# Query norms kept as token columns, and the sliding attention's query projections moved ahead of its units

## What is computed

```python
def _rms_norm(x, g):
    y = x * lax.rsqrt(jnp.mean(x * x, axis=-1, keepdims=True) + 1e-6)
    return y * g

# layer 0: two attentions with 16 query heads of 64 channels, causal, 512 keys
aq = _rms_norm(aq, qn_a); ak = _rms_norm(ak, kn_a)
bq = _rms_norm(bq, qn_b); bk = _rms_norm(bk, kn_b)
logits = q . k * HEAD_DIM ** -0.5 - slope[h] * dist      # -inf where dist < 0
p = softmax(logits)

# layer 1: sliding attention, 16 query heads, 4 key heads, window of 128, a sink per head
q = _rms_norm(q, qn_c); k = _rms_norm(k, kn_c)
logits = q . k * HEAD_DIM ** -0.5 - slope[h] * dist      # dist in 0..127
p = softmax(concat([logits, sink]))[..., :-1]
```

## Time and profile before

| | us |
|---|---|
| three runs | 2853.36, 2854.61, 2854.35; median 2854.35 |
| the profiled execution's own time | 2861.86 |
| its span, first to last instruction | 2860.1 |
| mean granted TensorE clock | 0.962 |
| busy share: PE, PEld, DVE, ACT, POOL | 94%, 75%, 41%, 37%, 43% |
| layer 0's projection and picks (VectorE's last pick ends) | about 50 to 266 |
| layer 0's attention | 266 to 381 |
| layer 1's chunk 6 projected | 863.23 |
| layer 1's units, first bias to the first matmul of the output projection | 869.46 to 998.20 |

### The profile page before, as it was taken

How to read it: one execution, slowest core, us unless ns; L and a number is a source line. 1 busy time by engine, 2 the same in 40 slices (tenths; PEclk the granted TensorE clock), 3 DMA queues, 4 the chain that set the end, 5 groups by cost and what they waited for, 6 DMA issues and landing times.

```text
span 2860.1 us, 34092 instructions
## 1 busy us (share of the span) xinstructions
PE 2682.9 (94%) x13037; PEld 2130.8 (75%) x13037; DVE 1175.7 (41%) x1698; ACT 1058.9 (37%) x1705; POOL 1235.3 (43%) x652
## 2 busy tenths in 40 slices
PE   6997889999998799999999999999999996999998
PEld 5665567888874478888788888888888762788886
DVE  3288633222147633221236655233321497433312
ACT  3332643332236533332345555333322322433321
POOL 2322533544433235444345655444444485344442
PEclk8998999999999899999999999999999997999998
DMA  8654512332320013323221211222322210132321
GB/s 270 215 167 143 175 45 74 97 108 92 98 75 30 30 59 103 103 88 102 82 74 59 74 60 53 93 91 92 99 96 96 69 64 15 61 116 88 99 96 55
DMA packets 275965, 265.14 MB, mean 93 GB/s; under 512 B 20268, under 2 KB 274829, under 8 KB 275853
## 3 DMA queue, kind: packets, MB, share of 16 engines
q1 hardware_dynamic: 275853, 263.59, 29.1%
HBM read 261.47 MB, written 2.10 MB: 92 GB/s over the span
## 4 chain that ended last, share of the span: by engine, by line
PE 80%; DVE 13%; ACT 3%; issue 2%; SPq 1%; POOL 0%; DMA 0%; DVEq 0%; ACTq 0%
PE bank L1240 20%; PE bank L1241 20%; PE bank L1242 20%; DVE bank L2364 3%; PE bank L980 1%; PE bank L982 1%; PE bank L981 1%; DVE score L2702 1%; PE bank L1264 1%; PE bank L971 1%; PE bank L973 1%; PE bank L972 1%; PE bank L1002 1%; PE bank L1266 1%; PE bank L1265 1%
## 5 line engine op out<-in xcount | busy, mean ns | idle before, releaser
L844 POOL TENSOR_TENSOR w_lo<-w_raw,w_hi 128x1024 fp32r<-128x1024 f32 (+1 forms) x364 | 863.7, 2382 | 1281.4 <-ACT w_hi L1875 746.1
L1240 PE MATMUL bank<-h_hi,w_hi 128*128 128x512 f32 x1632 | 643.8, 394 | 19.1 <-DVE h_lo L2513 12.4
L1241 PE MATMUL bank<-h_lo,w_hi 128*128 128x512 f32 x1632 | 639.5, 392 | 0.0
L1242 PE MATMUL bank<-h_hi,w_lo 128*128 128x512 f32 x1632 | 639.1, 392 | 0.0
L1875 ACT ACTIVATE w_hi<-w_raw 128x1024 fp32r<-128x1024 f32 (+1 forms) x232 | 233.2, 1019 | 482.5 <-PE bank L1242 437.5
L1240 PEld LDWEIGHTS bank<-h_hi,w_hi 128*128 128x128 f32 x1632 | 309.5, 190 | 88.8 <-issue 19.6
L1241 PEld LDWEIGHTS bank<-h_lo,w_hi 128*128 128x128 f32 x1632 | 309.3, 190 | 65.7 <-issue 1.7
L1242 PEld LDWEIGHTS bank<-h_hi,w_lo 128*128 128x128 f32 x1632 | 309.1, 189 | 64.9
L1240 PE MATMUL bank<-a_hi,w_hi 128*128 128x512 f32 x704 | 273.9, 389 | 0.0
L1241 PE MATMUL bank<-a_lo,w_hi 128*128 128x512 f32 x704 | 273.9, 389 | 0.0
L1242 PE MATMUL bank<-a_hi,w_lo 128*128 128x512 f32 x704 | 273.9, 389 | 0.0
(11 more groups left out here) (369 smaller groups left out, 4362.2 us busy)
## 6 DMA issues: line engine op xcount, KB each, us to landing
ada_w<-in_ada_w_dram SPq DMA_DIRECT2D x96, 512.0 KB, 6.1
w_raw<-in_ffn_gate_dram SPq DMA_DIRECT2D x22, 1024.0 KB, 5.2
w_raw<-in_ffn_up_dram SPq DMA_DIRECT2D x22, 1024.0 KB, 5.3
w_raw<-in_ffn_w_gate_dram SPq DMA_DIRECT2D x22, 1024.0 KB, 5.3
w_raw<-in_ffn_w_up_dram SPq DMA_DIRECT2D x22, 1024.0 KB, 5.2
w_raw<-in_ffn_down_dram SPq DMA_DIRECT2D x16, 1024.0 KB, 5.1
w_raw<-in_ssm_w_in_dram SPq DMA_DIRECT2D x16, 1024.0 KB, 5.2
w_raw<-in_ffn_w_down_dram SPq DMA_DIRECT2D x16, 1024.0 KB, 4.9
```

Of the source, the lines that this page charges most:

```text
L844: pool.tensor_tensor(w_lo[parity][:, 0:nk, half], w_raw[parity][:, 0:nk, half], w_hi[parity][:, 0:nk, half].bitcast(F32), ALU.subtract).th ...
L1240: pe.matmul(dst[m][:], hi, src_hi(k0 + k), start=first and k == 0, stop=False)
L1241: pe.matmul(dst[m][:], hi, src_lo(k0 + k), start=False, stop=False)
L1242: ins = pe.matmul(dst[m][:], lo, src_hi(k0 + k), start=False, stop=last and k == nk - 1)
```

## The change

The query norms are no longer applied to the queries. ScalarE copies the raw chunk times the gain (which holds the factor -1/8) into the query tile, which frees the bank (`q_copied`, `o_copied`). TensorE sums the squares with the tokens on the partitions: four pieces of the squares are stationary, two columns of the ones move, and the result is 128x8 (four token tiles by two heads). ScalarE takes the root of 128x8 into `q_sigma`. VectorE makes -1/sigma (`q_minus`) and slope times sigma, in four small instructions. In the units the bias is scaled by the column slope times sigma, the exp takes the column -1/sigma as its scale, and one more VectorE instruction on 128x2 rescales the minimum. Keys are treated as before. In layer 1 all chunks 7 to 11 are projected ahead of the unit loop, their squares, roots and splits too, and nothing of them is left in it. The sums of a query chunk are now written to the chunk's own bank, behind its copy. The columns lie where `log_decay` lies, which is used much later.

```diff
-                low_half(6)
+                for j in range(6, 12):
+                    low_half(j)
                 for s in range(U):
                     even_out(s)
-                    for j in o_ends(s):
-                        low_half(j)
...
             def sums(j):
-                take(2, o_root, j + 1)
+                b = 2 if j < KV_HEADS else O_BANK[j]
+                take(b, o_root, j + 1)
                 pe.wait_ge(o_squared, j + 1)
-                pe.matmul(bank[2][:], head_ones[:], sq[j % 2][:], start=True, stop=True).then_inc(o_summed, 1)
+                if j < KV_HEADS:
+                    pe.matmul(bank[b][:], head_ones[:], sq[j % 2][:], start=True, stop=True).then_inc(o_summed, 1)
+                    return
+                for i in range(NT):
+                    ins = pe.matmul(bank[b][:, 2 * i:2 * i + 2], sq[j % 2][:, P * i:P * i + P], head_ones[:, 0:P:HD],
+                                    start=True, stop=True)
+                ins.then_inc(o_summed, 1)
...
                 if k == 0:
-                    take(b, o_normed, j + 1)
+                    take(b, o_copied, j - 3)
                     pe.wait_ge(w_split, 2 * n + m + 1)
...
             def scores(u):
                 hp, i, w = o_tile(u)
                 k0 = P * max(i - 1, 0)
-                pe.wait_ge(o_normed, 5 + hp)
+                pe.wait_ge(o_normed, KV_HEADS)
+                pe.wait_ge(o_copied, hp + 1)
...
             sums(2)
-            half_cm(n0 + 3, 0, take(O_BANK[4], o_normed, 5))
+            half_cm(n0 + 3, 0, take(O_BANK[4], o_copied, 1))
             sums(3)
-            half_cm(n0 + 3, 1, take(O_BANK[5], o_normed, 6))
+            half_cm(n0 + 3, 1, take(O_BANK[5], o_copied, 2))
             sums(4)
-            half_cm(n0 + 4, 0, take(O_BANK[6], o_normed, 7))
+            half_cm(n0 + 4, 0, take(O_BANK[6], o_copied, 3))
             sums(5)
+            for j in range(7, 12):
+                for f in range(8 * (j - 7), 8 * (j - 7) + 8):
+                    query_part(f)
+                sums(j - 1)
+            sums(11)
             for s in range(U + O_LAG + 1):
-                fill = list(range(o_upto(s), o_upto(s + 1)))
                 if s < U:
                     scores(s)
-                for f in fill[:1]:
-                    query_part(f)
                 if O_LAG <= s < U + O_LAG:
                     turn(s - O_LAG)
-                for f in fill[1:]:
-                    query_part(f)
-                if s == 0:
-                    sums(6)
-                for j in o_ends(s - 1):
-                    sums(j)
                 if O_LAG + 1 <= s < U + O_LAG + 1:
                     weigh(s - O_LAG - 1)
...
                     pe.wait_ge(sq_ready, z + 1)
+                    if 1 <= r - qk_root0 <= 8:
+                        for i in range(NT):
+                            ins = pe.matmul(bank[4][:, 2 * i:2 * i + 2], sq[z % 2][:, P * i:P * i + P], head_ones[:, 0:P:HD],
+                                            start=True, stop=True)
+                        ins.then_inc(sq_summed, 1)
+                        return
                     pe.matmul(bank[4][:], head_ones[:], sq[z % 2][:], start=True, stop=True).then_inc(sq_summed, 1)
...
-                            if part[m] == "qk":
+                            if part[m] == "q":
+                                dst.append(take(banks[m], q_copied, qk + m))
+                            elif part[m] == "qk":
                                 dst.append(take(banks[m], qk_normed, qk0 + qk + 1 + (m if part[0] == "qk" else 0)))
...
-            EVEN_PARTS = [("qk", "plain"), ("bv",), ("plain", "plain"), ("plain", "plain"), ("qk", "qk"), ("qk", "qk"),
-                          ("qk", "qk"), ("qk", "qk"), ("qk", "qk"), ("qk", "qk"), ("tok", 256), ("tok", 256)]
+            EVEN_PARTS = [("qk", "plain"), ("bv",), ("plain", "plain"), ("plain", "plain"), ("q", "q"), ("q", "q"),
+                          ("q", "q"), ("q", "q"), ("qk", "qk"), ("qk", "qk"), ("tok", 256), ("tok", 256)]
...
                 act.activation(sq[j % 2][:], bank[O_BANK[j]][:], ACT.Square).then_inc(o_squared, 1)
+                if j >= KV_HEADS:
+                    act.activation(cq[:, j - 4, :], bank[O_BANK[j]][:], ACT.Copy, scale=qk_gain[:, 4:5]).then_inc(o_copied, 1)
                 round_half(n + 2, m)
 
             def root_of(j):
                 act.wait_ge(o_summed, j + 1)
+                if j >= KV_HEADS:
+                    act.activation(q_sigma[:, j - KV_HEADS, :], bank[O_BANK[j]][:, 0:2 * NT], ACT.Sqrt, bias=eps_col[1e-6][:],
+                                   scale=1.0 / HD).then_inc(o_root, 1)
+                    return
...
                 for t_ in range(2):
                     c = (2 * u + t_) % 32
-                    act.activation(o_prob[u % 4][:, w * t_:w * t_ + w], o_neg[u % 3][:, w * t_:w * t_ + w], ACT.Exp, scale=-1.0,
+                    act.activation(o_prob[u % 4][:, w * t_:w * t_ + w], o_neg[u % 3][:, w * t_:w * t_ + w], ACT.Exp,
+                                   scale=q_minus[:, hp, 2 * i + t_:2 * i + t_ + 1],
                                    bias=least[:, c // 16, c % 16:c % 16 + 1],
                                    accum_out=total[:, c // 16, c % 16:c % 16 + 1]).then_inc(o_exp, 1)
...
             root_of(5)
+            for j in range(7, 12):
+                square(j)
+                root_of(j - 1)
+            root_of(11)
             for s in range(U + O_LAG + 1):
                 if O_LAG <= s < U + O_LAG:
                     copy_turned(s - O_LAG)
-                if s == 1:
-                    root_of(6)
-                for j in o_ends(s - 1):
-                    root_of(j)
                 if s >= O_LAG + 1:
                     round_y(s - O_LAG - 1)
                 if s < U:
                     prob_exp(s)
-                for j in o_ends(s):
-                    square(j)
...
+                    if 1 <= j <= 8:
+                        act.activation(q_sigma[:, j - 1, :], bank[4][:, 0:2 * NT], ACT.Sqrt, bias=eps_col[1e-6][:], scale=1.0 / HD
+                                       ).then_inc(root_done, 1)
+                        return
...
                             act.activation(sq[z % 2][:], bank[b][:], ACT.Square).then_inc(sq_ready, 1)
+                            if part[m] == "q":
+                                to, g = (bq[:, qk - 1, :], 2) if qk <= 4 else (aq[:, qk - 5, :], 0)
+                                act.activation(to, bank[b][:], ACT.Copy, scale=qk_gain[:, g:g + 1]).then_inc(q_copied, 1)
...
-                link(dve.reciprocal(root[j % 2][:], root[j % 2][:]))
-                if j < KV_HEADS:
+                if j >= KV_HEADS:
+                    hp = j - KV_HEADS
+                    link(dve.reciprocal(q_minus[:, hp, :], q_sigma[:, hp, :]))
+                    dve.tensor_scalar(q_minus[:, hp, :], q_minus[:, hp, :], -1.0, None, ALU.mult)
+                    by_head = q_sigma[:, hp, :].rearrange("p (i t) -> p i t", t=2)
+                    for t_ in range(2):
+                        ins = dve.tensor_scalar(by_head[:, :, t_], by_head[:, :, t_], slope[2 * hp + t_], None, ALU.mult)
+                else:
+                    link(dve.reciprocal(root[j % 2][:], root[j % 2][:]))
                     ins = dve.scalar_tensor_tensor(out=ck[:, j, :], in0=bank[b][:], scalar=qk_gain[:, 5:6], in1=root[j % 2][:],
-                                                   op0=ALU.mult, op1=ALU.mult)
-                else:
-                    ins = dve.scalar_tensor_tensor(out=cq[:, j - 4, :], in0=bank[b][:], scalar=qk_gain[:, 4:5], in1=root[j % 2][:],
                                                    op0=ALU.mult, op1=ALU.mult)
                 ins.then_inc(o_normed, 1)
...
+                dve.wait_ge(o_normed, 5 + hp)
...
                 for t_ in range(2):
-                    ins = dve.scalar_tensor_tensor(out=neg[:, w * t_:w * t_ + w], in0=dist_i, scalar=slope[2 * hp + t_],
+                    ins = dve.scalar_tensor_tensor(out=neg[:, w * t_:w * t_ + w], in0=dist_i, scalar=q_sigma[:, hp, 2 * i + t_:2 * i + t_ + 1],
                                                    in1=bank[o_score_banks(u)[t_]][:, 0:w], op0=ALU.mult, op1=ALU.add)
                 ins.then_inc(o_biased, 1)
                 dve.wait_ge(o_biased, u + 1)
                 c = (2 * u) % 32
                 lc = least[:, c // 16, c % 16:c % 16 + 2]
                 link(dve.tensor_reduce(lc, neg[:, 0:2 * w].rearrange("p (t k) -> p t k", t=2), AX_X, ALU.min))
+                link(dve.scalar_tensor_tensor(out=lc, in0=lc, scalar=-1.0, in1=q_minus[:, hp, 2 * i:2 * i + 2], op0=ALU.mult,
+                                              op1=ALU.mult))
                 dve.tensor_tensor(lc, lc, neg_sink[:, 2 * hp:2 * hp + 2], ALU.min).then_inc(o_least, 1)
...
-            for j in range(6):
+            for j in range(12):
                 normed(j)
             for s in range(U + O_LAG + 1):
                 if s < U:
...
```

(30 more changed lines are left out.)

## The result

The changed kernel is slower. Its median is 2873.3 us (seven runs, 2870.4 to 2876.1) beside 2857.1 us for the kernel before (seven runs, 2853.4 to 2864.3), a ratio of 1.0054 with a 95% interval of 1.0042 to 1.0065. A second set of its runs gave 2871.0 us and 1.0048 (1.0035 to 1.0060). The forecast was 2847.3 us, range 2839 to 2860.

The account below looks back on a forecast made before the run. TensorE was taken as bound (busy 94% of the span), VectorE's work paid in a few stages only. Layer 1 gains 7.3 us, layer 0 gains 1.6 and loses 1.9: 2854.35 - 7.0 = 2847.3 us, range 2839 to 2860.

Parts of the forecast that it names:

- rival 2: Layer 1's loop: clock stays at half where values are made, costing 18 us instead of 3, total 2862; chance 0.13.
- signs that I named: Prediction wrong if steps average over 2.6 us, bank waits far exceed 2.3, or attention grows over 5 us.
- The chunks ahead, to 904.9: Layer 1 ahead of the loop: first bias moves from 869.46 to 904.9, adding 35.4 us.
- 3 x (2.3 + 5.50): Layer 1, chunks 9 to 11: each waits 2.3 us for its bank, then takes 5.50 us of products.
- The sum in the loop, 71.3 us: Layer 1's unit loop: steps of 2.23 or 2.02 us, 0.34 more with `low_y`, 71.3 us to the last bias.
- The column scalars replace constants; I cost them at nothing: Layer 1's unit loop: scalars read from columns instead of constants add no time.
- The clock in the loop, 3 us: Layer 1's loop: half clock slows two of twelve steps with values by 1.5 us each; bounds 0 and 18.
- Layer 0's projection, -1.6 us: Ahead of layer 0's attention: VectorE starts the A keys at 193.46 instead of 195.03, gaining 1.6 us.
- Layer 0's attention, +1.9 us: Layer 0's 32 units: the added 128x2 instruction, 0.19 us each, is paid in a third, losing 1.9 us.
- ten units: Layer 0's attention: ten of 32 units have the added instruction on the path, an estimate between the ends.
- Rival 3: Layer 0's attention: added instruction, held up by GpSimd, costs 8.8 us instead of 1.9, total 2854.2; chance 0.17.
- Held up by GpSimd: Layer 1: new VectorE instructions wait for GpSimd's splits, 2.4 us ahead of the loop, 0.15 per 128-key step.

Follow-up runs that it names:

- banks experiment: Changed kernel with chunks 7 to 11 in banks 7, 3, 4, 0 and 1, so none waits for an earlier root: 2858.8 us, ratio 1.0004 to before.
- fed loop: Changed kernel with idle TensorE products in layer 1's unit loop, three per step without values, one with: 2864.6 us, ratio 1.0028 to before.
- its part alone: Kernel before with only layer 1's edits, query chunks ahead of the units and column scalars: 2860.7 us, ratio 1.0017.
- layer 0's part alone: Kernel before with only layer 0's edits, token-column query norms, column scalars and the added 128x2 instruction: 2865.0 us, ratio 1.0023.

## Why the prediction was wrong

**Direction.** I gave slower by over 0.2% a chance of 0.10 and by one mechanism, rival 2. It came by others. By the runs of each part alone layer 1 cost 4.9 us where it was to gain 7.3, and layer 0 cost 6.6 where it was to cost 0.3. Three steps of the sum failed: dense products that a short wait slows (put at nothing ahead of the loop), column scalars "at nothing", and code behind the change taken to keep its time. Of the signs that I named only the attention's growth by over 5 us showed: steps took 2.46 us on average, under 2.6, and each wait 2.53. Step by step:

- *The chunks ahead, to 904.9.* From the end of chunk 6 that is 41.7 us; 45.6 were measured (871.17 to 916.73). Chunks 7 and 8 with their sums took 12.76 us (forecast 12.6), each wait 2.53 (2.3), the end of chunk 11 to the first bias 5.3 (5.7). The step that failed is "3 x (2.3 + 5.50)": after a wait the dense products themselves ran slower, 7.19 us in two of three chunks, 3.4 of the 3.9 us missing. The earlier trace rows had shown half clock after a gap in the loop, and I charged it there, not here, where all of TensorE's time is on the path. The banks experiment puts waits and slow products together at 8.4 us.
- *The sum in the loop, 71.3 us.* 76.4 were measured. "The column scalars replace constants; I cost them at nothing" failed: 0.12 us in each 256-key step (2.39 against 2.27), some 3.3 us in 31 steps. No row of before had a bias or an exp with such a scalar, and I gave the unknown no bounds. The added instruction was 0.19 us in most steps, as forecast (2.27 against 2.08). Hold-ups in 128-key steps, charged at 0.15, did not happen: 1.86 instead of 2.02. "There are 12 such steps of 256 keys" was a slip too: nine of the twelve steps with values have 256 keys, three have 128.
- *The clock in the loop, 3 us.* Right, and for the reason given: 2.4 us by the fed loop, 1.8 of them in two steps with values. Its extent was not as forecast: 38.8 of 76.4 us were at 0.5, but steps without values hid it, and of the steps with values most were at full clock. Rival 2's 18 us did not come.
- *Together*, layer 1 was to gain 7.3 us; it gained 1.1 in the trace, and the runs of its part alone are 4.9 us slower than before.
- *Layer 0's projection, -1.6 us.* -0.3 were measured. The A key's reciprocal came at 197.25; less 3.5 us of later start-up that is 193.8, as forecast (193.5). Of the rest, 1.0 us went into the end of a pick, held up by a split of GpSimd for longer than before.
- *Layer 0's attention, +1.9 us.* This is the largest miss of the sum: +8.0 in the pair of profiles. In the traces the old code took 108.3 to 115.7 us in seven kernels (mean 111.6), the new one 117.0 to 123.1 in six (mean 119.9): +8.3 us, and by the runs of layer 0's part alone +6.6 (4.0 to 9.1). The step that failed is again the scalars at nothing: at like clock the edit cost 4 to 5 us and the instruction 0 to 2 of it. Whether "ten units" on the path was wrong as well stays open (0.9 to 6.0 us by the runs, 6.1 if all units paid). The rest goes with the clock, which stood at 0.5 for 27 to 44 us in the new code and 16 to 33 in the old; whether the change brings that or the moment at which the stage begins, no run shows. Rival 3 named the place and 8.8 us, but for another reason: GpSimd held the new instruction up in five of 32 units, up to 0.61 us, 1.2 us in all (2.0 in the kernel's second profile), not 0.18 us in each.
- *Held up by GpSimd.* Right for both new kinds: 2.02 us for the `tensor_scalar`, 1.89 for the `scalar_tensor_tensor`. By the rule of the Trainium skill on the shared pair of ports (SBUF — State Buffer, "SBUF: two separate sides") this was to be so, and the trace agrees: both ended within 0.04 us of GpSimd's split. The 2.4 us ahead of the loop were paid, the 0.15 in each 128-key step was not.
- *The base.* I carried the median of three runs, 2854.35; that of 33 runs is 2856.5. The forecast was 2 us too low by that.
- *Unchanged code.* I took it to cost nothing. In this kernel's two profiles it cost 7.3 us behind layer 1, by the moment at which it begins. Nothing in the trace of before tells that moment, and hardly its size: its two SwiGLU stages with the same counts of instructions took 313.1 and 311.8 us. The range had no room for it.

**What the question should have been.** I asked whether the change as a whole gains. The move ahead alone is worth 15 us, and token columns alone in layer 1 some 11 (ratio 0.9960) to 14 by medians. Together, in the change's two banks, they are worth nothing, since both take the same 25 us of norms out of the loop: once the chunks are ahead, the columns save mostly what was already hidden and charge most of the 31 steps 0.35 us (76.4 against 64.5 us in the traces, 1.8 of it the two long steps). The earlier trace rows would have told it: a norm of 4.1 us is shorter than a chunk's 5.5 us of products. The banks are the other half of the loss. Ahead, steps and tail together took 134.9 us before, 118.0 with columns alone, 117.9 with the chunks ahead alone in five banks, 126.1 with both in five banks and 133.0 to 133.8 with both in two. So even in five banks both together are 8 us worse than either alone.

## What to carry to other kernels

When two edits remove the same cost, price each alone and then both: the second may only add its own overhead to every step. When dense work is moved to where nothing runs beside it, count its PSUM banks first, since a short wait between bursts is paid twice, once as a wait and once as slower products behind it. A scalar that turns from a constant into a column is an edit with a price: bound it, above all in an engine that sets the pace. And compare stages of two profiles at like time at 0.5, or a difference of the clock is taken for one of the edit.

## What the runs showed of the hardware

- A column as scalar costs per instruction, whatever its length here: 60 ns in VectorE's bias (443 to 503, 550 to 609, and 382 to 444 in layer 1), 92 ns in ScalarE's exp (558 to 650; 473 to 566 in layer 1). With constants instead both are back within 2 ns.
- The same instructions take different times by when they begin: 792.1 to 799.7 us for SwiGLU and Mamba mixer, 108.3 to 115.7 us for the old attention with 16 to 33 us of it at the lower of the two clock levels (1.2 instead of 2.4 GHz). Two idle products ahead of such code (they put off the output projection by 0.58 us) took 7.2 us off it. The Trainium skill (TensorE: Matmul & The Clock Gate, section "What's actually happening") says that the chip's judging runs freely and does not start anew with a kernel. The traces agree: in the same stage the clock fell 33.4 us from its start in one kernel and 36.4 in another.
- A wait of 1.58 us between bursts of dense products was followed by half clock over part of the next burst in two of three cases (chunks 9 and 10); without the wait the whole path ahead had 0.5 us of it.
- The new 128x2 instruction was held up until GpSimd's split ended (1.89 us). GpSimd's work on the weights holds it up too where it is under way: in five of layer 0's 32 units by 0.06 to 0.45 us. In layer 1's units of the changed kernel it took 160 ns each time, but there it met GpSimd only in six, and in the last 0.1 us of its instruction.
